# A two-layer transformer trunk: the down projection of each feed-forward block, 16 of its 22 input strips by seven block products per pair of output strips

## What is computed

```python
def _swiglu(h, w_gate_up, w_down):
    gu = h @ w_gate_up
    g, u = jnp.split(gu, 2, axis=-1)
    return (jax.nn.silu(g) * u) @ w_down

    # in reference(), for each layer i
    x = x + mix.astype(x.dtype)
    h = _rmsnorm(x, norm_ffn[i])
    x = x + _swiglu(h, ffn_w_gate_up[i], ffn_w_down[i]).astype(x.dtype)
```

## Time and profile before

| | us |
|---|---|
| median of three runs (2330.71 to 2332.80) | 2330.88 |
| the profiled execution, its own time | 2331.4 |
| its span, first to last instruction | 2329.6 |
| TensorE busy in the span | 2255.2 (97%) |
| VectorE, ScalarE, GpSimd busy | 1198.5, 854.2, 567.6 |
| matmuls of the gate and up stages, 2 x 22 x 7 x 12 | 3696 |
| matmuls of the down stages, 2 x 8 x 2 x 22 x 3 | 2112 |

### The profile page before, as it was taken

The page is one execution under the profiler, slowest core; times in us unless marked ns, Lnnn a source line. Parts: engine busy times, 40 slices in busy tenths (PEclk is TensorE's granted clock), DMA queues, the critical chain, the costliest instruction groups (busy, mean ns, idle before and its releaser), DMA issues.

```text
span 2329.6 us, 32539 instructions
## 1 busy us (share of the span) xinstructions
PE 2255.2 (97%) x11512; PEld 1839.1 (79%) x11512; DVE 1198.5 (51%) x1885; ACT 854.2 (37%) x1526; POOL 567.6 (24%) x423
## 2 busy tenths in 40 slices
PE   7998898999999999999999999999899999999998
PEld 6876686888888788877888777778688888878887
DVE  5659568444444434337332476646844444443432
ACT  3127334333333312222221477733433333331223
POOL 2423332222232000110000366643222222200011
PEclk9999998999999999999999999999999999999999
DMA  7340441322221613223442877544122222162312
GB/s 230 98 105 2 154 154 33 96 87 82 81 81 63 246 56 131 90 74 117 145 153 99 219 178 179 138 153 146 37 90 87 87 88 81 63 230 72 131 48 79
DMA packets 253241, 261.20 MB, mean 112 GB/s; under 512 B 15968, under 2 KB 221024, under 8 KB 248176
## 3 DMA queue, kind: packets, MB, share of 16 engines
q1 hardware_dynamic: 242160, 220.32, 31.8%
q10 hardware_dynamic: 11008, 39.92, 4.4%
HBM read 187.92 MB, written 65.08 MB: 109 GB/s over the span
## 4 chain that ended last, share of the span: by engine, by line
PE 89%; DVE 6%; DMA 2%; ACT 1%; POOL 1%; issue 1%; SPq 0%; ACTq 0%; DVEq 0%
PE psum L1713 12%; PE psum L1714 12%; PE psum L1715 12%; PE psum L1983 11%; PE psum L1985 11%; PE psum L1987 11%; PE psum L1861 3%; PE psum L1886 3%; PE psum L1961 2%; PE psum L1963 2%; PE psum L1962 2%; PE psum L1821 1%; PE psum L1822 1%; DVE b_full L1453 1%; DVE set_lo L1472 1%; DVE b_lo L1438 1%
## 5 line engine op out<-in xcount | busy, mean ns | idle before, releaser
L1983 PE MATMUL psum<-b_hi,a_hi 128*128 128x512 f32 x1232 | 484.6, 393 | 20.6 <-DVE b_lo L1438 20.6
L1987 PE MATMUL psum<-b_hi,a_lo 128*128 128x512 f32 x1232 | 482.7, 392 | 0.0
L1985 PE MATMUL psum<-b_lo,a_hi 128*128 128x512 f32 x1232 | 482.6, 392 | 0.0
L1983 PEld LDWEIGHTS psum<-b_hi,a_hi 128*128 128x128 f32 x1232 | 233.4, 189 | 72.5 <-issue 24.1
L1713 PE MATMUL psum<-set_hi,dw_hi 128*128 128x512 f32 x704 | 274.8, 390 | 3.2 <-DVE set_lo L1472 3.2
L1714 PE MATMUL psum<-set_lo,dw_hi 128*128 128x512 f32 x704 | 273.9, 389 | 0.0
L1715 PE MATMUL psum<-set_hi,dw_lo 128*128 128x512 f32 x704 | 273.9, 389 | 0.0
L1985 PEld LDWEIGHTS psum<-b_lo,a_hi 128*128 128x128 f32 x1232 | 233.5, 190 | 48.6 <-issue 0.5
L1987 PEld LDWEIGHTS psum<-b_hi,a_lo 128*128 128x128 f32 x1232 | 233.3, 189 | 49.0
L782 POOL TENSOR_TENSOR a_sum<-a_raw 128x512 f32<-128x512 f32 x88 | 114.6, 1302 | 501.2 <-DVE a_lo L1433 442.7
L748 POOL TENSOR_TENSOR score<-score,inv_l 128x128 f32<-128x128 f32 (+7 forms) x128 | 144.9, 1147 | 355.6 <-DVE inv_l L1319 353.9
(11 more groups left out here) (205 smaller groups left out, 3604.0 us busy)
## 6 DMA issues: line engine op xcount, KB each, us to landing
a_raw<-in_ffn_w_gate_up SPq DMA_DIRECT2D x88, 512.0 KB, 5.1
hid_scr<-hid_out SPq DMA_DIRECT2D x44, 512.0 KB, 5.7
set_full<-hid_scr SPq DMA_DIRECT2D x22, 1024.0 KB, 6.2
x_t<-x_scr SPq DMA_DIRECT2D x16, 1024.0 KB, 8.3
dw_raw<-in_ffn_w_down SPq DMA_DIRECT2D x32, 512.0 KB, 3.8
x_scr<-x_t ACTq DMA_DIRECT2D x24, 512.0 KB, 2.6
w_raw<-in_fox_w_in SPq DMA_DIRECT2D x22, 512.0 KB, 4.0
w_raw<-in_swa_w_out SPq DMA_DIRECT2D x16, 512.0 KB, 4.1
```

Source lines behind the costliest of these rows:

```text
L1983: T.matmul(out_ps, a_hi[i][:, j, :], b_hi[i][:, j, :], start=not more and j == 0, stop=False, skip_group_check=True)
L1985: T.matmul(out_ps, a_hi[i][:, j, :], b_lo[i][:, j, :], start=False, stop=False, skip_group_check=True)
L1987: last = T.matmul(out_ps, a_lo[i][:, j, :], b_hi[i][:, j, :], start=False, stop=j == KH - 1, skip_group_check=True)
```

## The change

The weights and the hidden values of strips 0 to 15 are taken as two groups of 8 strips (`DG` = 2). In a group, the output strips 2p and 2p+1, the even and odd hidden strips and the two token halves make a two-by-two by two-by-two block product with blocks of 4 strips. It takes seven products i = 0 to 6 for each of four pairs w, 12 matmuls each: 56 products per layer (`DP`), counted c = 28g + 4i + w. The mixed weights are made by GpSimd (`down_sums`) in 16 sums per group. The mixed hidden blocks are made by VectorE in the gate and up stage, four subtractions for each of the first eight pairs of hidden strips (`hidden_mixed`), and go to DRAM (`t_scr`) as 1 MB per pair. Weights use the seven slots `a_hi`, `a_lo` of gate and up, hidden blocks four slots of `b_hi`, `b_lo`. Strips 16 to 21 (`D_REST` = 6) are added by the old chunks. Products accumulate in two chains of four banks; after each product VectorE adds its bank to one half of one strip of `x_t`.

```diff
-FF_GROUPS = (8, 6, 8)
+DG = 2
+DSTEPS = 7 * DG
+DP = 4 * DSTEPS
+D_REST = FT - KD * DG
...
+        D_PAIRS = (3, 0, 1, 2)
+        D_SET_TICK = (33, 35, 37, 45, 51, 52)
+        D_W_TICK = (53, 54)
+        D_CHAIN = (0, 1, 0, 1, 1, 0, 1)
+        D_BEFORE = {2: 0, 3: 1, 4: 3, 5: 2, 6: 4}
+        D_TO = ((0, 0), (0, 0), (1, 1), (0, 1), (1, 1), (0, 1), (1, 0))
...
+            def store_t(layer, i):
+                sp.wait_ge(t_made, 4 * (KH * DG * layer + i + 1))
+                sp.dma_start(t_scr[:, bass.ds(i, 1), :], t_out[:, :, :].rearrange("p j n -> p (j n)").unsqueeze(1))\
+                    .then_inc(t_stored, 16)
...
+            def down_weight_high(layer, c):
+                g, i, w = d_split(c)
+                if c >= NP:
+                    act.wait_ge(d_prod, DP * layer + c - NP + 1)
+                else:
+                    act.wait_ge(*prod_at(FT * layer + FT - 1, c))
...
+                nc.scalar.activation(a_hi[c % NP][:, :, :], d_operand(g, i, w), ACT.Copy).then_inc(d_ahigh, 1)
+            def down_block_high(layer, n):
+                act.wait_ge(d_block_in[n % 4], d_loads(layer, n))
+                nc.scalar.activation(b_hi[D_SLOT[n]][:, :, :], d_full[D_SLOT[n]][:, :, :], ACT.Copy).then_inc(d_bhigh, 1)
...
+            def hidden_mixed(layer, r, i):
+                n, (even, odd) = 4 * (KH * DG * layer + i), hid_out
+                dve.wait_ge(hid_done, 2 * (r + 1))
+                wait(dve, t_stored, 16 * (KH * DG * layer + i))
+                V.tensor_tensor(t_out[:, 0, :], even[:, half(1)], even[:, half(0)], ALU.subtract).then_inc(t_made, 1)
+                V.tensor_tensor(t_out[:, 1, :], odd[:, half(1)], even[:, half(1)], ALU.subtract).then_inc(t_made, 1)
+                dve.wait_ge(t_made, n + 1)
+                V.tensor_tensor(t_out[:, 2, :], odd[:, half(1)], t_out[:, 0, :], ALU.subtract).then_inc(t_made, 1)
+                dve.wait_ge(t_made, n + 3)
+                V.tensor_tensor(t_out[:, 3, :], odd[:, half(0)], t_out[:, 2, :], ALU.subtract).then_inc(t_made, 1)
+                dve.wait_ge(t_made, n + 4)
...
+            def down_dve(layer, c0):
+                base = DP * layer
+                for c in range(DP):
+                    g, i, w = d_split(c)
+                    row, h = D_TO[i]
+                    m = 2 * D_PAIRS[w] + row
+                    if c < 4:
+                        dve.wait_ge(x_ffn[D_PAIRS[w]], 16 * (layer + 1))
+                    dve.wait_ge(d_prod, base + c + 1)
+                    wait(dve, d_add, base + c - 3)
+                    V.tensor_tensor(x_t[:, m, half(h)], d_bank(c), x_t[:, m, half(h)], ALU.add).then_inc(d_add, 1)
+                    if c % 4 == 2 and c // 4 + 2 < DSTEPS:
+                        down_block_low(layer, c // 4 + 2)
+                    if c + NP < DP:
+                        down_weight_low(layer, c + NP)
...
+            def down_products(layer):
+                base, last = DP * layer, FT * layer + FT - 1
+                for c in range(DP):
+                    g, i, w = d_split(c)
+                    n = 7 * g + i
+                    if w == 0:
+                        pe.wait_ge(d_blow, DSTEPS * layer + n + 1)
+                    pe.wait_ge(d_alow, base + c + 1)
+                    if i in D_BEFORE:
+                        pe.wait_ge(d_add, base + 28 * g + 4 * D_BEFORE[i] + w + 1)
...
+                    for j in range(KH):
+                        T.matmul(d_bank(c), a_hi[c % NP][:, j, :], b_hi[at0][:, j, :], start=begin and j == 0, stop=False,
+                                 skip_group_check=True)
...
```

378 lines of the change are left out of this document (254 added, 124 removed).

## The result

The changed kernel takes **2280.55 us** (median of four runs, 2277.91 to 2282.88) against 2330.8 of the kernel before on the same chip, a ratio of 0.978 (95% interval 0.977 to 0.980). The forecast was 2284.0, the range 2281 to 2295: the direction and the size came out as written, and the time lies 0.45 us under the range. The question of the experiments is therefore where 3.45 us of unforeseen gain come from, and how near the stage stood to the losses that were feared.

The account below looks back on a forecast made before the run. TensorE, busy 97% of the span, was taken as the bound: 2331.4 - 43.5 (matmuls) - 5.4 (old start loss) + 2.0 (new start) = 2284.5, less 0.5 for the median, 2284.0 us; range 2281 to 2295.

Parts of the forecast that it names:

- Matmuls: Down stages: 960 matmuls for 1056 per layer, 192 fewer over both at 0.2267 us each, 43.5 us less.
- The old start loss: Start of down: TensorE's waits for the first set's low parts disappear, 5.4 us less for both layers.
- First product: Start of down: hidden block 0 is split at 781.6, TensorE asks at 782.8; margin 1.2 us, no stall.
- Third block: Ninth down product: block 2, split behind additions awaiting `x_t`, is ready at 802.1, asked for at 804.6; margin 2.5 us.
- The charge of 2.0 us: Start of down: 1 us per layer added for the two narrow margins, bounds 0 and 5 us per layer.
- VectorE in steady down: Four-product steps in down: VectorE needs 7.8 us of TensorE's 10.88, so it fits; no charge.
- the meetings of the earlier trace: Down: a VectorE split with two SBUF operands beside a GpSimd sum takes 1.77 us for 0.69, 1.1 us per meeting.
- The rule of the Trainium skill: Down: GpSimd sums could hold VectorE 1.29 us each, 16 times per group, making 75 of 76 us.
- The backlog: VectorE in down: up to 5 us builds up and is worked off within each seven-step group; no loss.
- VectorE as the bound: Rival, chance 0.07: GpSimd meetings in every sum leave VectorE's backlog not worked off in down, 2298 to 2320 us.
- Mixed blocks and the stages behind down: Gate and up's extra subtractions, 2.8 us eight times per layer, cost nothing; the next stage's start stays.
- no loss at all: Low end of the range: no time lost at the down starts gives 2281.9; the range begins at 2281.

Follow-up runs that it names:

- b_count: The kernel before with 96 matmuls of each layer's down projection left out and no mixing work added: 2287.84 us, ratio 0.981.
- a_late: The changed kernel with the fourth 1 MB load of the residual tile moved ahead of the first mixed hidden block in SyncE's queue: 2291.14 us, ratio 0.9826.
- a_early: The changed kernel with the first two mixed hidden blocks loaded earlier and output pairs taken in the order 3, 2, 0, 1: 2282.99 us, ratio 0.979.
- a_dve2: The changed kernel with every second weight-block split from the ninth product on made twice on VectorE, 24 more operations per layer: 2291.56 us, ratio 0.9824.
- b_mix: The kernel before with the mixed-block subtractions and their 1 MB stores added in gate and up, read by nothing: 2330.4 us, ratio 0.9992.

## Why the prediction was right, and where it failed

**Matmuls, 43.5 us.** Right: b_count alone gives 21.7 us per layer, and 960 matmuls take 217.60 us, 0.22667 each, in the product form too.

**The old start loss, 5.4 us.** Right, if a little small: 2.71 and 2.74 in the execution that I read, 3.0 in each layer of b_count.

**First product.** The margin was put at 1.2 us and measured as 0.25 (L0) and 0.13 (L1). Its step was sound to a microsecond: from the store's issue at 770.91 ScalarE has block 0 at 783.22, 12.3 us, where the sum gave 11.4. VectorE could take it at 785.17. In a_late a 1 MB load ahead of it, 2.7 us by the working, cost 2.2 and 2.3.

**Third block.** The margin was put at 2.5 us and measured at 0.5 in L0 (split done at 809.0, asked for at 809.47) and below 0 in L1. The additions waited for `x_t` until 802.90 and 806.11, in the changed kernel's VectorE timeline:

```profile
802.90 0.69 DVE L1676 TENSOR_TENSOR x_t<-psum,x_t 128x512 f32<-128x512 f32 x1 [5.11 <-DMA x_t<-x_scr]
...
806.11 0.69 DVE L1676 TENSOR_TENSOR x_t<-psum,x_t 128x512 f32<-128x512 f32 x1 [1.92 <-DMA x_t<-x_scr]
```

From the first product's start these are 15.2 and 18.4 us, where the working had 13.6 and 16.3.

**The charge of 2.0 us** for both was twice too large: 0.0 and 0.96 us in this execution, 1.2 in all in each of the next two. The term was mis-sized by 1.0 us.

**VectorE in steady down.** 7.8 us of a step of 10.88 was worked out, 72%; measured are 82% over the 152 us. The groups of the changed kernel's blocks of L0 (busy, mean ns, idle before), against the earlier trace rows:

```profile
L1676 DVE TENSOR_TENSOR x_t<-psum,x_t 128x512 f32<-128x512 f32 x55 | 37.7, 685 | 26.3 <-PE psum L2253 19.2 <-DMA x_t<-x_scr 7.0
L1663 DVE TENSOR_TENSOR b_lo<-d_full,b_hi 128x2048 fp32r<-128x2048 f32 x13 | 32.9, 2530 | 0.0
L1656 DVE TENSOR_TENSOR a_lo<-a_sum,a_hi 128x512 fp32r<-128x512 f32 x24 | 23.5, 978 | 0.0
L1656 DVE TENSOR_TENSOR a_lo<-d_even,a_hi 128x512 fp32r<-128x512 f32 x15 | 10.2, 684 | 0.0
```

The additions, with one operand in PSUM, keep their 685 ns. The splits of `a_sum` grew from 688 to 978 ns in the mean, those of `d_even`, none of which meets a sum, did not. The 978 mixes two kinds: 11 of the 24 overlap a sum and take 1330 ns, the other 13 take 681. So the meetings of the earlier trace rows are there as forecast, and VectorE runs without a pause from 806.11 until it has caught up at 858.64. Of the two groups of seven blocks, 76 us each, the first took it 66.5 us (of 788 to 864) and the second 58.0; I had 72 at most. The place that matters lies in the first. The rule of the Trainium skill ("SBUF — State Buffer", section Who interferes with whom) agrees in kind; the 75 of 76 us worked out from it were not reached, since only 18 of the 53 weight splits and 6 of the 13 block splits in the window met a sum.

**The backlog** was put at up to 5 us and absorbed "since weight splits are seven products ahead". It was 7 us (the sixteenth product ends at 787.71 + 43.52 = 831.23, its addition starts at 838.35), and no loss is right. Some 2.5 us of it go away with an earlier order of the loads (a_early). But the reserve that holds it is not that of the splits: it is the addition four products back, 8.2 us. The prediction named it and gave it no number. By that number the margin is 0.6 us at the seventeenth product and 0.4 or nothing at the twentieth, and a_dve2 turned it into a loss of 5 to 6 us per layer. The chance of 0.07 for VectorE as the bound was drawn from shares; that no loss came was nearly luck, the stage being less than one weight split (0.69 us) away from it.

**Mixed blocks and the stages behind down.** Right: no cost in b_mix; the next stage starts 0.23 us after the last down matmul.

**The number and the range.** The 3.45 us between 2284.0 and 2280.55 split so: 1.0 is the charge. 1.6 are the untouched part, 986.6 us in the execution that the sum was made against and 985.0 in that of the changed kernel. 0.1 is gate and up, and 0.2 go back for the time outside the span (1.8 us before, 2.0 after). The rest, 0.8, is that the median lay 1.3 us under the profiled execution, and 0.5 was allowed. **The step that failed is the low end of the range:** "a little below no loss at all (2281.9)" (2282.0 by its own terms) takes everything outside the two stages as fixed, to a microsecond, from one execution. In 14 executions that part went from 978.5 to 988.3 us with a median of 984.4, and 986.6 is the third longest. By their median the same sum would have given 2281.8, and no loss at all 2279.7, with some 4 us of spread to either side: the range should have begun near 2276. The three runs of before, 2.1 us apart, hid it. The term of the sum that was mis-sized besides is the charge, 2.0 for the 1.0 measured; with 1.0 in its place the forecast is 2283.0, still 2.5 us above the median.
